# Gate projections of tiles 2 to 7 as seven block products per pair of tiles, with the low parts on GpSimd

## The chip, the cores and the metric

The kernel runs on one core of one Trainium2 chip. The metric is the device time of one execution in microseconds, the median of several; lower is better. A core has TensorE (PE in the rows, its weight loads PEld), VectorE (DVE), ScalarE (ACT), GpSimd (POOL), and SyncE (SP), whose queue here only issues transfers.

## The reference, cut to what matters

One decoder layer on 520 tokens (512 of a prompt, 8 single samples): three token mixers on one normalised input, merged by sigmoid gates, then an MLP with squared ReLU. The gates are the last 3 x 1024 columns of the input projection:

```python
def in_projection(h, norm_g, w_in, b_gate):
    xn = rmsnorm(h, norm_g)
    parts = jnp.split(xn @ w_in, SPLIT_POINTS, axis=-1)
    gates = tuple(jax.nn.sigmoid(parts[9 + i] + b_gate[i]) for i in range(N_BRANCH))
...
mixed = gates[0] * y_a + gates[1] * y_b + gates[2] * y_c
h = h + mixed @ w_out
hn = rmsnorm(h, norm_mlp_g)
return h + jnp.square(jax.nn.relu(hn @ w_up)) @ w_down
```

## The kernel before, in words

**Numbers.** Everything is float32, and TensorE gets each operand as two parts: a high (the value rounded to TensorE's format, an ACTIVATE Copy on ScalarE) and a low (value minus high). A block product is then three matmuls for each 128 x 128 weight block: high x high, high x low of the activation, low x high of it. The activation's parts are xh and xl, [128, 8 blocks, 520 tokens].

**Units and ticks.** A unit is one weight tile of 1024 x 128 (make_units, L51). It is loaded into one of WR = 3 raw slots (wraw), split by split_hi (L880) on ScalarE into one of two high slots (whi) and by split_lo on GpSimd (L836) or VectorE (L1209) into one of two low slots (wlo); LO decides which engine, in the gates and branches mostly in turn. A tick is one output tile for one half of the tokens (260), so two ticks a unit in the gates: 8 blocks x 3 = 24 matmuls into one of three PSUM banks G0 to G2 (BANK, L187). The branch units have shorter ticks: a "c" unit eight of 6 matmuls (yc of four tiles), an "ab" unit four of 12 (ya and yb of one tile). TICKS (L100) is the order, and each engine runs through the same list with its own part of each tick: TensorE project (L1712), VectorE take (L1308), ScalarE gate (L931) and others. make_plan (L290) hangs the attention's steps, the page loads of the cache and the branch splits on ticks by hand. Engines meet only at semaphores; within an engine the order of the list holds.

**Around the gates.** Tick 84 is the first gate tick (g0, tile 0, half 0). Gates come by tile, three branches each: units 42 to 53 are tiles 0 to 3. Then come "c" of tiles 0 to 3, and "ab" of tile t, each followed by the three gate units of tile t + 4; then "c" of tiles 4 to 7, and four "ab" units in a row; then eight "out" units. For a gate tick VectorE multiplies the bank by rstd into tg, and ScalarE takes the tanh in place. A branch tick of VectorE multiplies the bank by (1 + gate) into macc or mtmp and adds mtmp to macc, and after yb mix_split (L1091) and a VectorE step make mixh and mixl, the operands of "out". branch_split (L1075, L1602) makes binh and binl, the operands of "c" and "ab", from ticks 95 to 100 on. In ticks 84 to 95 TensorE also does sums over cached pages (v_sum) and smaller attention steps. x_again (L767) loads the input again into hT, to which "out" adds.

**Seven products.** In three quarters of the MLP's down projection the kernel already computes a pair of tiles as seven products instead of eight: product (L1688), with block sums on VectorE (block_sum, L1282), highs of 128 x 512 on ScalarE, three lows on GpSimd (plain_low, L850, those of unsummed blocks) and four on VectorE (sum_low), and take_product (L1256). It cuts the two tiles and the activation into 2 x 2 blocks (rows of the weights by 512, tokens by 260) and uses four sums of weight blocks and four of activation blocks.

## Time and profile before

| | us |
|---|---|
| median of 3 runs (1008.74 to 1009.38) | 1008.75 |
| the profiled execution | 1010.09 |
| its span, first to last instruction | 1006.8 |
| TensorE busy | 986.1 |
| VectorE busy | 587.9 |
| ScalarE busy | 439.8 |
| GpSimd busy | 312.6 |

Busy times are of the span. Durations on TensorE overlap, since matmuls are pipelined: a group's mean is longer than the distance between two matmuls, and the distance is to be taken from the chain or the timeline. The chain of waits goes back from the last instruction to what released it.

### The profile page before, as it was taken

Reading aid. Unit: us, or ns where it says so; the run is one execution under the profiler, and the core shown is the slowest. Engines: PE = TensorE matmul, PEld = TensorE weight load, DVE = VectorE, ACT = ScalarE, POOL = GpSimd, SP = SyncE. Lnnn points to the kernel's source line nnn. Section 1 sums busy time; section 2 is a strip of 40 time slices with the busy share of each in tenths; the row PEclk is TensorE's granted clock in tenths of the full one; section 3 lists DMA queues with packets and bytes.
Section 4 is the critical chain, followed back from the end, with each engine's and each line's share of the span. In section 5 each row is a group of like instructions: output and inputs, shape, how many; then the busy total and the mean of one; then the engine's idle time right before and its main releaser. Section 6 shows DMA issues by size and latency. Waiting matters only on the chain.

```text
span 1006.8 us, 21775 instructions
## 1 busy us (share of the span) xinstructions
PE 986.1 (98%) x8426; PEld 914.7 (91%) x8426; DVE 587.9 (58%) x1042; ACT 439.8 (44%) x858; POOL 312.6 (31%) x180
## 2 busy tenths in 40 slices
PE   7999999999999999999999999999999999999996
PEld 7988787797787787899999999999999999999995
DVE  6214478799355556253444475777847947873334
ACT  6114656677244332252233324465346436424532
POOL 2333233222312221012211112244634445354720
PEclk9999999999999999999999999999999999999999
DMA  8589977756797676624222326537576586469102
GB/s 301 181 274 320 336 260 237 289 204 207 264 334 238 224 241 202 241 84 169 89 101 85 105 89 226 204 138 266 218 262 257 215 282 250 159 261 359 61 1 85
DMA packets 65671, 209.47 MB, mean 208 GB/s; under 512 B 7833, under 2 KB 10138, under 8 KB 63266
## 3 DMA queue, kind: packets, MB, share of 16 engines
q1 hardware_dynamic: 65282, 207.75, 58.7%
q8 instruction: 67, 1.10, 0.4%
q10 hardware_dynamic: 288, 0.35, 0.2%
q14 instruction: 34, 0.28, 0.1%
HBM read 200.59 MB, written 51.48 MB: 250 GB/s over the span
## 4 chain that ended last, share of the span: by engine, by line
PE 93%; DVE 4%; issue 1%; ACT 1%; DMA 0%; DVEq 0%; ACTq 0%
PE G L1658 61%; PE S L1658 14%; PE Z L1658 13%; PE TR L1661 2%; PE OU L1658 2%; DVE pw L1496 1%; DVE mtmp L1201 1%; DMA xraw<-in_xt_dram 0%; DVE macc L1198 0%; DVE psp L1201 0%; PE TR L1658 0%; DVE share L1547 0%; DVE dvT L1198 0%; ACT mixh L878 0%; DVE pT L1505 0%
## 5 line engine op out<-in xcount | busy, mean ns | idle before, releaser
L1658 PE MATMUL G<-xh,whi 128*128 128x260 f32 x1288 | 372.3, 289 | 7.9 <-DVE xl L1201 7.2
L1658 PE MATMUL G<-xl,whi 128*128 128x260 f32 x1288 | 364.7, 283 | 0.0
L1658 PE MATMUL G<-xh,wlo 128*128 128x260 f32 x1288 | 364.4, 283 | 0.0
L844 POOL TENSOR_TENSOR wlo<-wraw,whi 128x1024 fp32r<-128x1024 f32 x60 | 148.4, 2474 | 477.2 <-ACT whi L878 477.2
L1658 PEld LDWEIGHTS G<-xh,whi 128*128 128x128 f32 x1288 | 243.5, 189 | 38.3 <-issue 32.3
L1658 PEld LDWEIGHTS G<-xl,whi 128*128 128x128 f32 x1288 | 243.7, 189 | 0.0
L1658 PEld LDWEIGHTS G<-xh,wlo 128*128 128x128 f32 x1288 | 243.6, 189 | 0.0
L878 ACT ACTIVATE whi<-wraw 128x1024 fp32r<-128x1024 f32 (+1 forms) x84 | 88.0, 1048 | 204.4 <-PE G L1658 186.0
L840 POOL TENSOR_TENSOR wlo<-mraw,whi 128x512 fp32r<-128x512 f32 x60 | 81.0, 1374 | 95.2 <-ACT whi L878 95.2
L854 POOL TENSOR_TENSOR mlow<-mraw,bhigh 128x512 fp32r<-128x512 f32 x36 | 57.9, 1626 | 66.0 <-DVE bsum L1198 58.9
L1198 DVE TENSOR_TENSOR tg<-G,rstd 128x260 f32<-128x260 f32 x48 | 20.5, 427 | 78.7 <-PE G L1658 78.7
L1198 DVE TENSOR_TENSOR slow<-bsum,bhigh 128x512 fp32r<-128x512 f32 x48 | 60.1, 1252 | 3.0 <-ACT bhigh L878 3.0
L1658 PE MATMUL S<-xl,whi 128*128 128x260 f32 x176 | 49.7, 282 | 0.0
L1658 PE MATMUL S<-xh,wlo 128*128 128x260 f32 x176 | 49.6, 282 | 0.0
L1658 PE MATMUL S<-xh,whi 128*128 128x260 f32 x176 | 49.6, 282 | 0.0
L878 ACT ACTIVATE whi<-mraw 128x512 fp32r<-128x512 f32 (+1 forms) x62 | 36.3, 637 | 25.6 <-PE G L1658 9.4
L1496 DVE TENSOR_TENSOR_SCAN pw<-psp 128x512 f32<-128x512 f32 (+3 forms) x33 | 46.4, 1406 | 1.1
L1658 PE MATMUL G<-binh,whi 128*128 128x260 f32 x160 | 45.7, 285 | 1.3 <-issue 1.3
L1658 PE MATMUL G<-binh,wlo 128*128 128x260 f32 x160 | 45.2, 283 | 0.0
L1658 PE MATMUL G<-binl,whi 128*128 128x260 f32 x160 | 45.2, 283 | 0.0
L878 ACT ACTIVATE bhigh<-bsum 128x512 fp32r<-128x512 f32 x48 | 30.2, 630 | 32.4 <-DVE bsum L1198 32.0
L936 ACT ACTIVATE tg<-tg,cvec 128x260 f32<-128x260 f32 x48 | 24.2, 505 | 45.6 <-DVE tg L1198 45.5
(329 smaller groups left out, 2227.9 us busy)
## 6 DMA issues: line engine op xcount, KB each, us to landing
wraw<-in_w_in_dram SPq DMA_DIRECT2D x65, 512.0 KB, 5.7
kv<-in_kpool_dram SPq DMA_DIRECT2D x128, 256.0 KB, 3.7
kv<-in_vpool_dram SPq DMA_DIRECT2D x128, 256.0 KB, 3.5
mraw<-in_w_up_dram SPq DMA_DIRECT2D x32, 512.0 KB, 5.7
out_win_k_kept_dram<-in_cache_win_k_dram SPq DMA_DIRECT2D x8, 2047.0 KB, 11.3
out_win_v_kept_dram<-in_cache_win_v_dram SPq DMA_DIRECT2D x8, 2047.0 KB, 11.5
mraw<-in_w_down_dram SPq DMA_DIRECT2D x30, 512.0 KB, 3.5
wraw<-in_w_ab_dram SPq DMA_DIRECT2D x8, 512.0 KB, 3.2
```

Of the source, the lines that this page charges most:

```text
L840: nc.gpsimd.tensor_tensor(low(u)[:, part], raw(u)[0][:, part], high(u)[:, part].bitcast(F32), ALU.subtract).then_inc(w_lo, 1)
L844: nc.gpsimd.tensor_tensor(low(u), raw(u)[0], high(u).bitcast(F32), ALU.subtract).then_inc(w_lo, 1)
L854: nc.gpsimd.tensor_tensor(block_low(g, j), block_raw(g, j), block_high(g, j).bitcast(F32), ALU.subtract).then_inc(b_lo_pool, 1)
L878: return nc.scalar.activation(out, in_, ACT.Copy, **kw)
L936: nc.scalar.activation(part, part, ACT.Tanh, scale=0.5, bias=bgate[:, g, t:t + 1]).then_inc(tanh_made, 1)
L1198: return nc.vector.tensor_tensor(out, a, b, op)
L1201: return nc.vector.scalar_tensor_tensor(out, a, scalar, b, op0, op1)
L1496: link(nc.vector.tensor_tensor_scan(w_[:, ::-1], l[:, ::-1], l[:, ::-1], carry, ALU.add, ALU.bypass))
L1658: return nc.tensor.matmul(out, lhsT, rhs, start=start, stop=stop, **kw)
L1661: return nc.tensor.transpose(out, in_, ident[0:rows, 0:rows])
```

## The change

Gate tiles 2 to 7 are taken in pairs of tiles (2 and 3, 4 and 5, 6 and 7) for each of three branches: nine pairs, in three batches of three. A pair is seven products of 12 matmuls; its last two come after the first product of the next pair. The first batch follows gate tile 1, the second "ab" of tile 1, the third "ab" of tile 3. ScalarE makes the seven highs of 128 x 512 in a ring of six, GpSimd all seven lows, VectorE four sums of weight blocks. Banks are shared: products 0, 2, 1, 5 follow each other in one bank, 3 and 6 in another, 4 has its own; ScalarE copies the first bank out after 0, 2 and 1, VectorE adds bank and copy and scales by rstd. Sums of the activation (xd1 to xd4, 128 x 1040 each) are made in ticks 85 to 96: six steps on GpSimd (x_odd), four on VectorE (x_even), four highs on ScalarE (x_hi) and four lows on VectorE (x_lo); the last pair overwrites a quarter of xh and xl. The branch splits 0 to 3 come ten ticks earlier, the page loads at the end of the attention every 2.5 ticks instead of 3, and x_again waits for the last gate product. Several tiles move in SBUF, which changes no instruction of theirs.

```diff
-    for t in range(4):
+    for t in range(2):
         gates(t)
+    gate_pairs(2)
     for half in range(2):
         unit("c", half, "w_c", half, KC, [("yc", 2 * i, 2, "dil", 4 * half + i) for i in range(4)])
         for t in range(4 * half, 4 * half + 4):
             unit("ab", t, "w_ab", t, KC, [("ya", 0, 4, "conv", t), ("yb", 4, 4, "sb", t)])
-            if half == 0:
-                gates(t + 4)
+            if t in (1, 3):
+                gate_pairs(t + 3)
...
+GSEQ = (0, 4, 2, 3, 1, 5, 6)
...
+            _seven = [(_u, ("gprod", 0, KC // 2, None, _q), _j, _j == 6) for _j in GSEQ]
+            TICKS += _seven[:1] + _late + _seven[1:5]
+            _late = _seven[5:]
...
+G_HIGHS, G_SUM_RING = 6, 6
...
+    if _q % 3:
+        _k = [gate_tick(_q - 1, n) for n in range(7)]
+        _ticks = (_k[1:7] + [_next], [_k[1], _k[1], _k[3], _k[4]], [_k[1], _k[2], _k[3], _k[4], _k[5], _k[6], _next])
+    elif _q == 0:
+        _ticks = ([_f - 3] * 3 + [_f - 2] * 2 + [_f - 1, _next], [_f - 4, _f - 4, _f - 3, _f - 3], [_f - 3, _f - 3, _f - 2, _f - 2, _f - 2, _f - 1, _next])
+    else:
+        _ticks = ([_f - 6, _f - 6, _f - 5, _f - 4, _f - 4, _f - 3, _next], [_f - 6, _f - 6, _f - 5, _f - 4], [_f - 6, _f - 6, _f - 5, _f - 4, _f - 4, _f - 3, _next])
...
-        v_ticks.append(v_ticks[-1] + 3)
+        v_ticks.append(v_ticks[-1] + 2.5)
...
+    for n in range(2):
+        add(t + 2.5 * n, "x_odd", n)
+        add(t + 3 + n, "x_even", n)
+    for n in range(3):
+        add(v_end + 3 + 0.5 * n, "x_hi", n)
+        add(v_end + 3 + 0.5 * n, "x_lo", n)
+    add(GATED_TICK - 0.5, "x_hi", 3)
+    add(GATED_TICK - 0.5, "x_lo", 3)
+    add(gate_tick(GPAIRS - 1, 6) + 1, "x_again")
...
+            def x_odd(n):
...
+                for i, (a, b, op) in enumerate(((ah, bh, ALU.subtract), (out, al, ALU.add), (out, bl, ALU.subtract))):
+                    if i:
+                        pool.wait_ge(xd_odd, 3 * n + i)
+                    nc.gpsimd.tensor_tensor(out, a, b, op).then_inc(xd_odd, 1)
...
+            def gate_low_pool(q, n):
+                j = G_POOL[n]
...
+                pool.wait_ge(g_hi, 7 * q + GSEQ.index(j) + 1)
...
+                nc.gpsimd.tensor_tensor(gate_low(q, j), gate_raw(q, j), gate_high(q, j).bitcast(F32),
+                                        ALU.subtract).then_inc(g_lo_pool, 1)
...
+            def gate_seven(k, q, j):
+                b, t = gate_tiles(q)
+                if j in (0, 2, 1):
+                    if j == 0 and b == 0:
+                        await_gate_parts(act, t)
+                    act.wait_ge(made, k + 1)
+                    copy(gate_part(t + (j > 0), b, j % 2), bank[BANK[k]][:, 0:HALF]).then_inc(g_copied, 1)
+                if j not in (0, 2, 3):
...
+                    nc.scalar.activation(part, part, ACT.Tanh, scale=0.5, bias=bgate[:, b, tile:tile + 1]).then_inc(tanh_made, 1)
+
+            def gate_hi(q, n):
+                j = GSEQ[n]
...
+                m = 7 * q + n - G_HIGHS
+                if m >= 0:
+                    act.wait_ge(made, gate_tick(m // 7, m % 7) + 1)
+                copy(gate_high(q, j), gate_raw(q, j)).then_inc(g_hi, 1)
...
+            def take_gate(k, q, j):
+                if j not in (4, 1, 5, 6):
+                    return
...
+                if j != 5:
+                    dve.wait_ge(g_copied, 3 * q + (4, 6, 1).index(j) + 1)
+                dve.wait_ge(made, k + 1)
+                if j == 5:
+                    tt(dst, src, root, ALU.mult).then_inc(dve_took, 1)
+                    return
...
+                tt(dst, src, dst, ALU.add).then_inc(dve_took, 1)
+                dve.wait_ge(*took(k))
+                tt(dst, dst, root, ALU.mult).then_inc(g_scaled, 1)
...
+            def gate_product(k, part, q, j):
+
+                if part == 0:
+                    pe.wait_ge(g_lo_pool, 7 * q + G_POOL.index(j) + 1)
+                    if q == 0 and j in (1, 2, 3, 6):
+                        pe.wait_ge(xd_lo, (2, 3, 6, 1).index(j) + 1)
+                    if j in (2, 1, 5):
+                        pe.wait_ge(g_copied, 3 * q + (2, 1, 5).index(j) + 1)
+                    elif j == 6:
+                        pe.wait_ge(*took(at("gprod", q, 1)))
+                    else:
+                        pe.wait_ge(*took(PREV[k]))
+                out = bank[BANK[k]][:, 0:HALF]
+                act_h, act_l = gate_act(j)
+                for kc in range(part * KC // 4, (part + 1) * KC // 4):
+                    wh, wl = gate_high(q, j)[:, kc, :], gate_low(q, j)[:, kc, :]
+                    mm(out, wh, act_h[:, kc, :], kc == 0 and j in (0, 4, 3), False, skip_group_check=True)
+                    mm(out, wh, act_l[:, kc, :], False, False, skip_group_check=True)
+                    ins = mm(out, wl, act_h[:, kc, :], False, kc == KC // 2 - 1, skip_group_check=True)
```

## Rows read from the trace of the kernel before

**Rows 1.** The page's sections 1 and 2: busy time by engine, granted clock.
```profile
PE 986.1 (98%) x8426; PEld 914.7 (91%) x8426; DVE 587.9 (58%) x1042; ACT 439.8 (44%) x858; POOL 312.6 (31%) x180
...
PEclk9999999999999999999999999999999999999999
```

**Rows 2.** Chain that ended last, in order of time: start us, us, what.
```profile
392.88 8.85 PE G L1658 x72
...
431.44 39.51 PE G L1658 x330
471.64 107.19 PE G L1658 x894
...
699.37 1.44 PE Z L1658 x12
```

**Rows 3.** Windows: stretch, us, busy (count) of PE, PEld, DVE, ACT, POOL, clock.
```profile
470.00:600.00 130.00, 128.66 (x1067) 127.80 (x1066) 70.81 (x123) 40.48 (x56) 26.36 (x11) 1.00 0.31 104
```

**Rows 4.** The same chain in the last four "ab" units.
```profile
582.93 0.42 DVE mtmp L1201
583.36 0.02 issue
583.38 0.44 DVE macc L1198
```

**Rows 5.** Groups of instructions by shape, 390 to 600: busy us, mean ns, idle before.
```profile
L844 POOL TENSOR_TENSOR wlo<-wraw,whi 128x1024 fp32r<-128x1024 f32 x17 | 40.7, 2392 | 174.5 <-ACT whi L878 174.5
...
L1198 DVE TENSOR_TENSOR tg<-G,rstd 128x260 f32<-128x260 f32 x48 | 20.5, 427 | 78.7 <-PE G L1658 78.7
L1198 DVE TENSOR_TENSOR macc<-macc,mtmp 128x260 f32<-128x260 f32 x32 | 19.7, 616 | 1.1
L1198 DVE TENSOR_TENSOR wlo<-wraw,whi 128x1024 fp32r<-128x1024 f32 x16 | 19.6, 1223 | 7.2 <-ACT whi L878 7.2
...
L1198 DVE TENSOR_TENSOR binl<-convy,binh 128x520 fp32r<-128x520 f32 x4 | 2.6, 695 | 1.1 <-ACT binh L878 1.1
...
L936 ACT ACTIVATE tg<-tg,cvec 128x260 f32<-128x260 f32 x48 | 24.2, 505 | 45.6 <-DVE tg L1198 45.5
```

**Rows 6.** Timeline of GpSimd, then of VectorE, 476 to 480.5: start us, us.
```profile
476.73 2.40 POOL L844 TENSOR_TENSOR wlo<-wraw,whi 128x1024 fp32r<-128x1024 f32 x1 [10.04 <-ACT whi L878]
...
477.49 1.92 DVE L1198 TENSOR_TENSOR macc<-macc,mtmp 128x260 f32<-128x260 f32 x1
479.44 0.42 DVE L1201 SCALAR_TENSOR_TENSOR mtmp<-tg,G 128x260 f32<-128x260 f32 x1
479.90 0.43 DVE L1198 TENSOR_TENSOR macc<-macc,mtmp 128x260 f32<-128x260 f32 x1
```

**Rows 7.** Timeline of VectorE, then of GpSimd, in a seven-product pair of the down projection.
```profile
697.50 0.69 DVE L1198 TENSOR_TENSOR bsum<-mraw,bsum 128x512 f32<-128x512 f32 x1
698.10 0.42 DVE L1198 TENSOR_TENSOR hT<-hT,Z 128x260 f32<-128x260 f32 x1
...
700.15 1.44 DVE L1198 TENSOR_TENSOR slow<-bsum,bhigh 128x512 fp32r<-128x512 f32 x1
...
701.86 1.44 DVE L1198 TENSOR_TENSOR slow<-bsum,bhigh 128x512 fp32r<-128x512 f32 x1
...
701.01 1.73 POOL L854 TENSOR_TENSOR mlow<-mraw,bhigh 128x512 fp32r<-128x512 f32 x1
```

**Rows 8.** Timeline of GpSimd in the up projection: two lows, VectorE not on SBUF.
```profile
743.37 2.56 POOL L840 TENSOR_TENSOR wlo<-mraw,whi 128x512 fp32r<-128x512 f32 x2 [3.17 <-ACT whi L878]
```

**Rows 9.** The page's section 5: the highs of the block sums on ScalarE.
```profile
L878 ACT ACTIVATE bhigh<-bsum 128x512 fp32r<-128x512 f32 x48 | 30.2, 630 | 32.4 <-DVE bsum L1198 32.0
```

**Rows 10.** Timeline: GpSimd's low of unit 44; VectorE's take of tick 95.
```profile
397.20 2.39 POOL L844 TENSOR_TENSOR wlo<-wraw,whi 128x1024 fp32r<-128x1024 f32 x1 [17.62 <-ACT whi L878]
...
434.45 0.43 DVE L1198 TENSOR_TENSOR tg<-G,rstd 128x260 f32<-128x260 f32 x1 [3.33 <-PE G L1658]
```

**Rows 11.** The page's section 6: issues, KB each, median us to landing.
```profile
wraw<-in_w_in_dram SPq DMA_DIRECT2D x65, 512.0 KB, 5.7
...
kv<-in_vpool_dram SPq DMA_DIRECT2D x128, 256.0 KB, 3.5
...
hT<-in_xt_dram SPq DMA_DIRECT2D x1, 2080.0 KB, 8.3
```

More of the change, by code:

```diff
@@ L189 @@
 FIRST, LEAD = 4, 4
-_opened = UP_TICK
+_opened = 3
+_free = [RING[(GATED_TICK + _n) % GBANKS] for _n in range(GBANKS)]
 for _k in range(NT):
@@ L211 @@
 for _u, _unit in enumerate(UNITS):
-    HI.append(sum(0 if seven(u) else 1 + halved(u) for u in range(_u + 1)))
-    if seven(_u):
+    HI.append(sum(0 if seven(u) or gated(u) else 1 + halved(u) for u in range(_u + 1)))
+    if seven(_u) or gated(_u):
         LO.append(None)
@@ new lines, in x_lo, with gate_sum @@
+            def x_lo(n):
+                dve.wait_ge(xd_hi, n + 1)
+                if n == 3:
+                    hi, lo, full_ = xh[:, 0:4, half(1)], xl[:, 0:4, half(1)], xd1
+                else:
+                    i = (1, 2, 0)[n]
+                    hi, lo, full_ = xdh[:, i], xdl[:, i], (xd2, xd3, xd4)[n]
+                tt(lo, full_[:], hi.bitcast(F32), ALU.subtract).then_inc(xd_lo, 1)
+            def gate_sum(q, n):
+                i = G_SUMS[n]
+                even, odd = raw(U_GATE[q]), raw(U_GATE[q] + 1)
+                top, end = slice(0, KC // 2), slice(KC // 2, KC)
+                if q == 0 and n == 0:
+                    dve.wait_ge(xd_lo, 3)
+                    dve.wait_ge(bin_lo, 4)
+                if n == 0:
+                    dve.wait_ge(*even[1:])
+                    dve.wait_ge(*odd[1:])
+                if q == 1 and n == 0:
+                    dve.wait_ge(bin_hi, 9)
+                m = 4 * q + i - G_SUM_RING
+                if m >= 0:
+                    dve.wait_ge(made, at("gprod", m // 4, SUM_AT[m % 4]) + 1)
+                if n:
+                    dve.wait_ge(g_summed, 4 * q + n)
+                first, second = gate_raw(q, SUM_AT[0]), gate_raw(q, SUM_AT[1])
+                a, b, op = ((odd[0][:, top], odd[0][:, end], ALU.add), (first, even[0][:, top], ALU.subtract),
+                            (even[0][:, top], odd[0][:, top], ALU.subtract), (even[0][:, end], second, ALU.subtract))[i]
+                tt(gate_raw(q, SUM_AT[i]), a, b, op).then_inc(g_summed, 1)
@@ L1371, in take @@
                     dve.wait_ge(made, k + 1)
-                    m = macc[:, tile, half(h)]
+                    m = macc[tile // 4][:, tile % 4, half(h)]
                     gate = tg[tile % 4][:, g, half(h)]
```

289 lines of the change are left out of this document (229 added, 60 removed).

## The prediction

> **What bounds the kernel now.** I read the page's busy times first: TensorE is busy for 98% of the span, GpSimd for 31%, and the granted clock is 0.9 or more in every slice [rows 1], which is the upper level, 2.4 GHz. Busy shares don't say who sets the end, so the chain of waits comes next, merged and in order of time: through the gates it is TensorE alone, 330 matmuls in 39.51 us and then 894 in 107.19 us without a break [rows 2]. That gives the price of one 128x128x260 matmul, 39.51/330 = 0.1197 us. The stretch 470 to 600 confirms it: TensorE 128.66 of 130 us, VectorE 70.81, ScalarE 40.48, GpSimd 26.36 [rows 3]. So here work removed from TensorE is time won, as long as three engines that are now half idle or more can carry what is put on them. The only place where the chain leaves TensorE is the run of four "ab" units at the end, where it sits on VectorE's mtmp and macc steps, 0.42 and 0.44 us apart [rows 4].
>
> **The edit on TensorE.** A pair of gate tiles is now 2 tiles x 2 token halves x 8 blocks x 3 = 96 matmuls; as seven products of 4 blocks x 3 it is 84. Nine pairs save 9 x 12 = 108 matmuls, 108 x 0.1197 = 12.9 us. Nothing is added on TensorE. That seven products can run at this price is seen in the down projection, 12 matmuls in 1.44 us [rows 2]. Within a pair TensorE then takes 84 x 0.1197 = 10.05 us instead of 11.5.
>
> **What the other engines get, per pair.** GpSimd: seven lows of 128x512 instead of one 128x1024 (the other of the pair is VectorE's). Alone such a low takes 2.56/2 = 1.28 us [rows 8]; seven are 9.0 us of the 10.05. ScalarE: seven highs of 0.63 us [rows 9], three copies of 128x260 (not in the trace; between the 0.39 that a high of this size would take in proportion and the 0.50 us of a tanh [rows 5]; I take 0.4) and four tanh, about 7.5 us; it fits, but only in order. VectorE loses a 1.22 us low and two multiplies, and gets four block sums of 0.69 [rows 7], four adds of 0.43 and three extra scalings of 0.43: about 6 us. By counts all fits. It fits badly because VectorE and GpSimd can't both work on SBUF.
>
> **The lock.** Look at GpSimd's low from 476.73 to 479.13 [rows 6] and at VectorE's macc<-macc,mtmp beside it: it takes 1.92 us, ends just after 479.13, and the same instruction right after takes 0.43 [rows 6]. The group's mean is 616 ns [rows 5]. The multiply of PSUM by rstd never shows this (mean 427 [rows 5]). In the seven-product stage it works both ways: VectorE's slow<-bsum,bhigh take 1.44 us, GpSimd's low 1.73 instead of 1.28, and one of each goes by every 1.71 us (700.15 to 701.86) [rows 7]. Two back-to-back sums are 0.60 apart (697.50, and the next instruction at 698.10), so I price a 128x512 VectorE step at 0.60 of a shared resource and a GpSimd low at 1.71 - 0.60 = 1.11. In the same manner: 1024 elements on GpSimd 2.39 - 0.15 = 2.25, 1040 elements 2.28, on VectorE 1.15 and 1.17 (from 1.22), 520 elements 0.65 and 260 elements 0.35 (from 695 and 430 ns) [rows 5, 6].
> The Trainium skill says the same thing of this pair in SBUF — State Buffer, "SBUF: two separate sides": the port pair that VectorE and GpSimd share is an exclusive lock, taken by a two-SBUF-input VectorE instruction or a GpSimd one for its whole length. The trace agrees (1.92 against 0.43 us). It speaks against this change, and GPSIMD Engine Reference, "Engine selection", does too, since it advises VectorE for elementwise work and calls GpSimd about twice as slow on two inputs (here 2.39 against 1.22 us). Without the lock the sum would be the whole 12.9 us.
>
> **Per pair the lock is overbooked**: 7 x 1.11 + 4 x 0.60 + 3 x 0.35 = 11.2 us against TensorE's 10.05. Only a lead, lows made before a batch of three pairs begins (at most six highs exist at once), can bridge that. So I count the lock over each batch.
>
> **Batch 1 with what leads to it.** The count begins when GpSimd starts the low of unit 44 at 397.20 [rows 10]. Until product 6 of the third pair can run, the lock must have served on GpSimd: two unit lows 4.5, x_odd 6 x 2.28 = 13.7, 21 lows 23.3, the low of the "c" unit, which stands before the last low, 2.25: 43.75 us. On VectorE: two unit lows 2.3, ten branch lows 6.5, x_even and x_lo 8 x 1.17 = 9.4, 12 sums 7.2, 8 scalings 2.8: 28.2 us. Together 72 us, so 469.2 at the earliest. TensorE ends the last tick of gate tile 1 at 434.4 [rows 10] and would want that product after 20 others and two short "yc" ticks, 28.7 + 1.4 later, at 464.6. Stall: at least 4.6 us. The bound from below takes a lock that never idles; it will idle while ScalarE and VectorE hand each other the ten branch splits and the x sums in ticks 91 to 96, and I add 1. The far end is some 5 us more.
>
> **Batches 2 and 3.** From six ticks of 12 matmuls (6 x 1.44 = 8.6 us) before a batch, where its first highs are due, to its last product there are 38.8 us. The lock needs 21 lows 23.3, 12 sums 7.2, 8 scalings 2.8, six macc adds 2.1, two mixl 1.3, one unit low 1.15: 37.9 us. It just fits. But two "ab" units now stand together ahead of each batch, and there VectorE has, in 8.6 us, six mtmp 2.5, six adds 2.6, two mixl 1.4 and four sums 2.7 = 9.2 us, with six lows (6.7 us of lock) to dodge: 9.2 + 6.7 - 8.6 - 2.9 (two banks of slack) = 4.4 us at worst, 0 at best. I take 1.5 for each batch, as the alternate pattern of [rows 7] hides about two thirds, and 0.4 for the short ticks behind batches 1 and 3.
>
> **Edits at nothing.** The weights keep three raw slots; a tile lands 5.7 us after issue [rows 11], an odd tile's slot comes free with the second low of the pair before, some 8 us ahead of its sum; if that cover goes, 1 us a pair. SyncE's load of hT now waits for the last gate product with weight loads behind it; 8.3 us [rows 11] lie under 28 us of "c" and "ab" work. Page loads at 2.5 instead of 3 ticks each land in 3.5 us [rows 11] under a step of 9. The moved tiles of the MLP cost nothing.
>
> **Sum.** 12.9 - (4.6 + 1.0) - 2 x 1.5 - 0.4 = 3.9 us won. The profiled execution took 1010.09 us (span 1006.8), so it would be 1006.2; it stands 1.3 above the median of the timed runs, 1008.75, and from that the forecast is **1004.9 us** (this case: 1001.5 to 1006.7).
>
> **Rivals.** (1) *The lead covers nearly all.* If a low holds the lock for less than 1.11, or VectorE slips into the 0.17 us that GpSimd leaves between two lows, batch 1 stalls 2 us or less: 996 to 1001, say 998. For it: the down stage keeps TensorE at 1.44 us per product with VectorE almost full. Against: only three lows per pair are GpSimd's there.
> (2) *No change.* The hand-overs of ticks 91 to 96 leave the lock idle longer: ScalarE must do x_hi 3 (over 1 us) before it can copy product 0's bank, which product 2 waits for; x_lo 3 must be done for product 1. With 4 us for that, 1008.9.
> (3) *Slower: ScalarE's order holds a bank.* After product 3 ScalarE goes to the high of the next pair's product 2, and stands there until VectorE's second sum. Behind product 4 VectorE has an add 0.43, a scaling and two sums, each of which may first wait 1.11 for a low: 0.43 + 1.46 + 1.71 + 1.71 = 5.3 us, against the 4.3 us of three products. So the copy of product 1's bank comes 1.0 + 0.63 + 0.4 = 2.0 us after its end, while product 5 wants the bank after 1.44: 0.6 a pair; product 4 of the next pair, whose bank frees with VectorE's take of product 5, adds 0.3. Nine pairs x 0.9 = 8 us: **1012.9**. It decides from 3.9/9 = 0.43 us a pair. For it: 11.2 us of lock per 10.05 means that VectorE's steps meet a low nearly each time. Against: in a batch's first pair GpSimd is capped by the ring of highs and leaves gaps.
> (4) *The lock alone*: a rule taken at its word, every pair at 11.2 us and no lead, wins 9 x (11.5 - 11.2) = 2.7 us less 5.6 for the x sums: 1011.7. It belongs to (3) in the chances; the Trainium skill's page on SBUF, as cited, is the rule.
> That the change doesn't do what it says can be left out: 84 matmuls a pair stand in the code.
>
> **Chances.** Forecast 0.33, rival (1) 0.15, (2) 0.20, (3) with (4) 0.32. A difference of 0.2%, 2 us, is about what a measurement of this kernel can tell from no change. Faster by more: 0.33 + 0.15 = 0.48; within: 0.20; slower: 0.32. The range cuts the upper half of (1) and the tail of (3), where all nine pairs wait 1.2 us or more: 998.5 to 1014. The likeliest case's own is 1001.5 to 1006.7.
>
> **What would show it.** 8318 matmuls instead of 8426. GpSimd's lows of 128x512 in the gates at 1.5 to 1.75 us each (1.3 would speak for rival 1). TensorE idle 4 to 7 us between 410 and 470, released by GpSimd's low or a VectorE step; under 2 us in products inside batches 2 and 3, over 4 us if rival 3 holds, then released by ScalarE's copy of G. The time from the first "out" tick to the end is unchanged. The prediction is wrong if TensorE has no gaps there, or if its gaps end with a weight load.

## The result, and the profile after

The changed kernel takes **1031.88 us** (median of 4 runs, 1030.99 to 1033.51) beside 1008.95 for the kernel before on the same chip: 1.0229 times as long, 95% interval 1.0211 to 1.0246. It is 22.9 us slower, where 3.9 us less had been forecast, and it lies outside the range. The saved matmuls are gone as counted, so 22.9 + 12.9 = 35.8 us were lost elsewhere.

The page, sections 1 and 2, as [rows 1]:

```profile
PE 983.5 (96%) x8318; PEld 906.9 (88%) x8318; DVE 663.6 (64%) x1104; ACT 467.7 (45%) x934; POOL 402.4 (39%) x240
...
PEclk9999999999999999999999999999999999999998
```

There are 8318 matmuls instead of 8426. TensorE's share fell by two points only, VectorE and GpSimd are still under two thirds, and nothing on this page looks like a bound. The windows tell more (columns: stretch, us, busy and count of PE, PEld, DVE, ACT, POOL, then clock, DMA share, GB/s). They are the lead-in with batch 1, one round of batch 2 with the two "ab" units behind it, and two short stretches; [rows 3] is a stretch of the same place before:

```profile
386.00:470.00 84.00, 74.29 (x598) 65.05 (x595) 65.14 (x68) 35.98 (x66) 48.67 (x26) 0.96 0.38 130
501.50:550.60 49.10, 43.66 (x349) 42.21 (x349) 38.72 (x53) 23.23 (x47) 33.18 (x22) 1.00 0.26 87
447.00:449.00 2.00, 1.28 (x6) 1.31 (x7) 1.66 (x2) 0.58 (x2) 0.69 (x1) 0.54 0.00 0
449.00:452.00 3.00, 3.00 (x21) 3.00 (x21) 2.83 (x5) 2.35 (x5) 1.27 (x1) 0.74 0.00 0
```

A round holds 348 matmuls, 41.7 us at 0.1197, and takes 49.1; VectorE is busy for 38.7 of them and GpSimd for 33.2. Behind the last gate product nothing changed: from the first matmul on mixh, the start of the "out" units, to the end of the span it is 409.3 us (from 619.97) against 409.6 (from 597.24).

**Where TensorE stood.** These are the first matmuls after its longest waits, in the timeline (start us, us, engine, what, count, idle before and who ended it): the first three products of batch 1, the "c" unit's second tick, and the first pair of batch 2 up to the ends of its pairs.

```profile
438.20 0.39 PE L1948 MATMUL G<-xh,ghigh 128*128 128x260 f32 x1 [1.55 <-POOL glow L1029]
...
442.11 0.36 PE L1948 MATMUL G<-xh,ghigh 128*128 128x260 f32 x1 [2.20 <-DVE tg L1424]
...
447.72 0.56 PE L1948 MATMUL G<-xdh,ghigh 128*128 128x260 f32 x1 [3.94 <-POOL gslow L1029]
...
479.44 0.36 PE L1948 MATMUL G<-binh,whi 128*128 128x260 f32 x1 [2.05 <-issue]
...
501.52 0.36 PE L1948 MATMUL G<-xh,ghigh 128*128 128x260 f32 x1 [0.81 <-DVE mtmp L1427]
...
505.90 0.36 PE L1948 MATMUL G<-xdh,ghigh 128*128 128x260 f32 x1 [1.24 <-ACT tg L1055]
...
511.57 0.39 PE L1948 MATMUL G<-xh,ghigh 128*128 128x260 f32 x1 [0.61 <-POOL glow L1029]
...
523.15 0.39 PE L1948 MATMUL G<-xh,ghigh 128*128 128x260 f32 x1 [0.90 <-POOL glow L1029]
```

Tick 95 ended at 434.4 before. After two products, 2.9 us, the third could start at 437.3; it starts at 447.72, 10.4 late: 2.2 had been lost when tick 95 ended (436.65), 7.7 are the three waits above. The rest of the ledger goes by the time between first matmuls, less 0.1197 us for each matmul between them. It is 1.3 us because the third product ran at the lower clock (the fourth starts 2.74 us after it instead of 1.44, with the 0.54 and 0.74 above), 5.3 in the rest of batch 1 and its "c" unit, 2.7 in the two "ab" units behind it, 7.4 in the round of batch 2, and 8.6 from there to the first "out" tick, where the kernel before loses 1.9 that are taken off. About 4 of these 8.6 belong to the second "c" unit (a wait of 2.1, then a clock of 0.69 to 0.93). Together that is 35.7 of 35.8, and each of batches 2 and 3, with the waits ahead of it, costs some 7.

**One pair at its steady pace.** GpSimd, then VectorE, then the high on ScalarE that GpSimd waits for at 527.54:

```profile
515.49 4.24 POOL L1029 TENSOR_TENSOR gslow<-gsum,ghigh 128x512 fp32r<-128x512 f32 x3 [1.29 <-ACT ghigh L1055]
519.72 5.07 POOL L1029 TENSOR_TENSOR glow<-wraw,ghigh 128x512 fp32r<-128x512 f32 x3
524.76 1.49 POOL L1029 TENSOR_TENSOR gslow<-gsum,ghigh 128x512 fp32r<-128x512 f32 x1
527.54 4.17 POOL L1029 TENSOR_TENSOR gslow<-gsum,ghigh 128x512 fp32r<-128x512 f32 x3 [1.29 <-ACT ghigh L1055]
```

```profile
518.50 1.78 DVE L1424 TENSOR_TENSOR gsum<-wraw 128x512 f32<-128x512 f32 x1
520.39 1.58 DVE L1424 TENSOR_TENSOR gsum<-gsum,wraw 128x512 f32<-128x512 f32 x1
522.07 1.57 DVE L1424 TENSOR_TENSOR gsum<-wraw,gsum 128x512 f32<-128x512 f32 x1
523.57 0.42 DVE L1424 TENSOR_TENSOR tg<-G,tg 128x260 f32<-128x260 f32 x1
524.02 1.06 DVE L1424 TENSOR_TENSOR tg<-tg,rstd 128x260 f32<-128x260 f32 x1
525.01 1.79 DVE L1424 TENSOR_TENSOR gsum<-wraw 128x512 f32<-128x512 f32 x1
```

```profile
526.83 0.63 ACT L1055 ACTIVATE ghigh<-gsum 128x512 fp32r<-128x512 f32 x1 [1.20 <-DVE gsum L1424]
```

From 515.49 to 527.54 is one pair: 12.05 us for TensorE's 10.05. (TensorE's own distance between two first products is 11.58 here, 511.57 to 523.15, since some lows were made ahead of the batch.) GpSimd is busy for 10.8 of the 12.05. Every sum of VectorE in this stretch, 0.69 us alone, takes 1.6 to 1.8, because it lets one low go first (over the round the three kinds of sum have means of 1.42, 1.28 and 0.99, so some meet none); the step that reads PSUM (523.57) takes its 0.42. The fourth sum, which may start only behind these, begins at 525.01 just behind a low's start, ends at 526.80, its high ends at 527.46, and for this GpSimd stands 1.29 us. The two engines take turns and then wait for each other once a pair.

### The profile page after: what moved, and what is told of

It reads as the page before. It is cut to its first block, busy times and chain, and to the rows that moved or that the text cites. A ratio compares the mean times of both kernels' runs of the same rounds, so it can differ in the third digit from the quotient of the medians.

```text
span 1029.2 us, 21949 instructions
## 1 busy us (share of the span) xinstructions
PE 983.5 (96%) x8318; PEld 906.9 (88%) x8318; DVE 663.6 (64%) x1104; ACT 467.7 (45%) x934; POOL 402.4 (39%) x240
## 4 chain that ended last, share of the span: by engine, by line
PE 80%; DVE 8%; issue 4%; POOL 4%; ACT 2%; DMA 1%; SPq 0%; DVEq 0%; ACTq 0%; POOLq 0%
PE G L1948 50%; PE S L1948 14%; PE Z L1948 11%; POOL gslow L1029 3%; PE TR L1951 2%; PE OU L1948 2%; DVE binl L1424 1%; POOL glow L1029 1%; DVE xd L1424 1%; DVE tg L1424 1%; ACT ghigh L1055 1%; DVE mtmp L1427 1%; DMA xraw<-in_xt_dram 1%; DVE pw L1784 1%; DVE wlo L1424 1%
## 5 line engine op out<-in xcount | busy, mean ns | idle before, releaser
L1948 PE MATMUL G<-xh,whi 128*128 128x260 f32 x992 | 289.6, 292 | 8.7 <-DVE xl L1427 7.4
L1948 PE MATMUL G<-xl,whi 128*128 128x260 f32 x992 | 282.0, 284 | 0.0
L1948 PE MATMUL G<-xh,wlo 128*128 128x260 f32 x992 | 281.6, 284 | 0.0
L990 POOL TENSOR_TENSOR wlo<-wraw,whi 128x1024 fp32r<-128x1024 f32 x51 | 128.3, 2515 | 359.6 <-ACT whi L1055 359.6
L1948 PEld LDWEIGHTS G<-xh,whi 128*128 128x128 f32 x992 | 188.4, 190 | 40.1 <-issue 32.9
L1948 PEld LDWEIGHTS G<-xh,wlo 128*128 128x128 f32 x992 | 188.4, 190 | 0.0
L1948 PEld LDWEIGHTS G<-xl,whi 128*128 128x128 f32 x992 | 188.4, 190 | 0.0
L1029 POOL TENSOR_TENSOR gslow<-gsum,ghigh 128x512 fp32r<-128x512 f32 x36 | 51.0, 1430 | 22.6 <-ACT ghigh L1055 13.7
L1948 PE MATMUL G<-xh,ghigh 128*128 128x260 f32 x144 | 42.6, 296 | 11.8 <-POOL glow L1029 5.8
L1029 POOL TENSOR_TENSOR glow<-wraw,ghigh 128x512 fp32r<-128x512 f32 x27 | 41.4, 1556 | 28.1 <-ACT ghigh L1055 25.0
```

Source lines behind the costliest of these rows:

```text
L990: nc.gpsimd.tensor_tensor(low(u), raw(u)[0], high(u).bitcast(F32), ALU.subtract).then_inc(w_lo, 1)
L1029: nc.gpsimd.tensor_tensor(gate_low(q, j), gate_raw(q, j), gate_high(q, j).bitcast(F32), ALU.subtract).then_inc(g_lo_pool, 1)
L1948: return nc.tensor.matmul(out, lhsT, rhs, start=start, stop=stop, **kw)
```

## The experiments

"Before" is the kernel before, measured beside each run on the same chip; its medians lie between 1008.61 and 1009.41. The differences to the kernel after that follow are between medians of separate sets of executions, mostly on another chip, so they are good to about 1 us. The first four runs had two executions each, the others four to six. All change the kernel after unless said otherwise.

| run | us | before | ratio (95%) |
|---|---|---|---|
| e1 lows on half | 1016.86 | 1008.82 | 1.005 to 1.011 |
| e2 small x sums | 1025.90 | 1008.82 | 1.014 to 1.020 |
| e3 four lows on VectorE | 1026.81 | 1008.82 | 1.015 to 1.021 |
| e4 x_odd on VectorE | 1028.68 | 1008.82 | 1.017 to 1.023 |
| e5 bank | 1024.91 | 1009.09 | 1.015 to 1.018 |
| e6 ring | 1029.08 | 1009.09 | 1.018 to 1.021 |
| e7 all mended | 1016.84 | 1009.09 | 1.006 to 1.010 |
| e8 tiles 4 to 7 | 1019.50 | 1009.09 | 1.009 to 1.012 |
| e9 early entry | 1035.25 | 1008.96 | 1.025 to 1.028 |
| e10 six, x sums spread | 1026.46 | 1008.96 | 1.016 to 1.022 |
| e11 six, pairs between | 1036.80 | 1008.96 | 1.026 to 1.030 |
| e12 nine, all and early | 1017.23 | 1008.96 | 1.006 to 1.010 |
| e13 copies for sums | 1029.94 | 1008.61 | 1.019 to 1.022 |
| e14 light | 1002.73 | 1008.61 | 0.993 to 0.997 |
| e15 v pages | 1030.43 | 1008.61 | 1.021 to 1.024 |
| e16 six, all mended | 1016.46 | 1009.41 | 1.005 to 1.008 |
| e17 three, all mended | 1013.65 | 1009.41 | 1.003 to 1.006 |

### How much hangs on GpSimd's lows and on the x sums

```diff
-gate_low(q, j), gate_raw(q, j), gate_high(q, j).bitcast(F32)
+gate_low(q, j)[:, 0:2], gate_raw(q, j)[:, 0:2], gate_high(q, j)[:, 0:2].bitcast(F32)
```

> The changed kernel (1031.9 us, 23 slower than the one before), but each of GpSimd's 63 gate lows works on half of its elements (128x256), and TensorE multiplies with the written half twice, so the low parts of these products are not right; matmuls, waits and order are as they were. Theory A (throughput: the lows hold the SBUF lock that VectorE and GpSimd share, 11.2 us for a pair of 10.05): a low falls from 1.11 to about 0.55 us of lock, a pair to 7.3, the waits of TensorE inside batches 2 and 3 (5.5 us each in the changed kernel's trace) nearly go: 31 to 36 us of stalls become about 20, so 1015 to 1019. Theory B (order: what TensorE waits for are hand-overs VectorE to ScalarE to GpSimd at a batch's start and the x sums ahead of the first): 1027 to 1030, since only the last link of each chain is 0.6 us shorter.

It leaves half of each low out (the products read the written half twice). 15.0 us came off, as theory A had it. Its round in the same window view:

```profile
498.84:542.91 44.07, 43.22 (x348) 42.09 (x349) 28.48 (x53) 23.43 (x47) 20.14 (x22) 1.00 0.29 96
```

44.07 us instead of 49.10, with VectorE's busy time down by 10.2 us although not one of its instructions changed: that was time in which it stood before GpSimd's lows. Batch 1's entry hardly moved: the third product starts at 447.12 instead of 447.72, after a wait of 4.1 us, and the profile names ScalarE's copy for it:

```profile
447.12 0.56 PE L1948 MATMUL G<-xdh,ghigh 128*128 128x260 f32 x1 [4.09 <-ACT tg L1055]
```

```diff
-nc.gpsimd.tensor_tensor(out, a, b, op).then_inc(xd_odd, 1)
+nc.gpsimd.tensor_tensor(out[:, :, 0:8], a[:, :, 0:8], b[:, :, 0:8], op).then_inc(xd_odd, 1)
```

The same for x_even, x_hi and x_lo: the sums of the activation cover 8 of 260 columns, and the products read x itself.

> The changed kernel with the steps that make the activation's block sums (six on GpSimd, four on VectorE, the highs and lows of the four) cut from 260 columns to 8 in each row; the products of the sums take other parts of the activation instead, so they are not right. Theory B (the lead-in): the third product starts 10.4 us late in the changed kernel, plus 1.5 us of lower clock behind it; both go except about 2 us: 1021 to 1023. Theory A: the lock has 23 us less to serve ahead of the first batch, but batches 2 and 3 stay as they are: 1022 to 1025 too; what tells them apart is the place, under A TensorE's waits for lows inside the first batch go as well (3 us more).

6.0 us less, outside the times of both theories (1021 to 1023, 1022 to 1025). The third product started at 441.48 instead of 447.72, still after a wait of 3.1 us. The place speaks for theory B: the waits for lows inside the first batch stayed (1.38 us at 460.65), and a round of batch 2 still took 49.1. The x sums cost 6 us in the place that the change gave them.

### Who does the lows

```diff
+for q, n in GLOW_DVE_AFTER.get(k, []):
+    gate_low_dve(q, n)          # lows of the sums 2, 3, 1, 5; GpSimd keeps 0, 4, 6
```

> The changed kernel with the four lows of summed blocks of each pair on VectorE, as in the down projection, and three on GpSimd. Theory A: VectorE holds the lock 0.60 us for a low and GpSimd 1.11, so a pair falls from 11.2 to 9.2 us of lock, under TensorE's 10.05: waits inside batches fall by a half or more, 1022 to 1026. Theory B: VectorE's list gets 36 steps longer, it is late already at each batch's start, and the copies and highs of ScalarE behind it come later: 1031 to 1036. No wait is added for TensorE but the one for a low by its new maker.

5.1 us less, 0.8 above theory A's range. By turns a pair would fall by 4 x (1.28 - 0.60) = 2.7 us, from 12.05 to under TensorE's 10.05, 18 us for nine; most of that didn't come. GpSimd now stood for ScalarE's highs for 93.6 us between 386 and 610 (its plain and sum lows together 50.7 in the kernel after), and product 0 of a pair still waited 0.6 for its low.

```diff
-nc.gpsimd.tensor_tensor(out, a, b, op).then_inc(xd_odd, 1)
+tt(out, a, b, op).then_inc(xd_odd, 1)       # x_odd among VectorE's stages
```

> The changed kernel with the six x_odd steps on VectorE (1.24 us each) instead of GpSimd (2.9 each). Theory A: 13.7 us of lock become 7.0, and VectorE's steps no longer wait for GpSimd's in ticks 85 to 91: the lateness of 10.4 us at the third product falls to 4 to 6, so 1026 to 1028. Theory B, order alone: VectorE has 7.4 us more to do in a stretch where TensorE waits for it: 1031 to 1036.

3.2 us less, 0.7 above theory A's range. The third product still waited until 445.44.

### Banks and rings

```diff
-            if _late and (_job[0] == "ya" or _h):
+            if _late:
```

> After kernel with one edit: the two late products (5, 6) of a batch's last pair stand behind the first yc tick of the c unit instead of the second, as they already do behind the first ya tick. Theory A (a held bank): at the c unit two of three banks belong to pending products, so the second yc tick must wait 2.3 to 2.4 us for VectorE's take of the first, in batches 1 and 3; with the edit both gaps go, and what the lowered clock costs behind them: 1032 - 4 to 5 = about 1027.5. Rival B (VectorE is simply behind there, since its sums and adds meet GpSimd's lows): the wait moves to another tick of the same place and the time falls by at most 1: 1031.

7.0 us less, more than theory A had: both waits at the "c" units are gone (4.2), and the clock behind the second stays at 1.00 (in the kernel after 0.69 from 586 to 589 and 0.93 from 589 to 600). What held the tick at 479.44 is seen on VectorE in the kernel after; the take of the first "yc" tick, macc, stands behind a unit's low, and the second tick has no other bank:

```profile
477.35 0.52 DVE L1424 TENSOR_TENSOR tg<-tg,rstd 128x260 f32<-128x260 f32 x1
477.79 1.21 DVE L1424 TENSOR_TENSOR wlo<-wraw,whi 128x1024 fp32r<-128x1024 f32 x1
478.93 0.41 DVE L1427 SCALAR_TENSOR_TENSOR macc<-tg,G 128x260 f32<-128x260 f32 x1
```

```diff
+    _ticks[0][6] = _k[6] if _q % 3 else _f      # the high of product 6, was _next
```

> After kernel with one edit: ScalarE makes the high of a pair's last product (6) one product earlier, behind product 6 of the pair before (in a batch's first pair behind product 0), instead of together with the high of the next pair's product 0. GpSimd's work and VectorE's are the same. Theory A (order): GpSimd idles for a high and then has two lows in a row before the next pair's product 0, which waits 0.9 to 1.2 us in each of the six second and third pairs; with the edit these gaps go, 5 to 7 us, about 1026. Rival B (the lock between VectorE and GpSimd is the bound of a pair, 11.2 us of lock to 10.05 of TensorE): no change beyond 1 us, 1031 to 1032.

2.8 us less, so theory A holds for a part only, and rival B's 1 us is passed too. The profiled execution was the slowest of the five (1034.04; the others 1027.86 to 1029.14), so its rows show where the waits stand and not where the 2.8 us were won. The waits moved: a round of batch 2 takes 48.64 us instead of 49.1, and the second pair's first product, released at 511.57 in the kernel after, no longer waits, but the third's waits longer than at 523.15:

```profile
526.88 0.39 PE L1949 MATMUL G<-xh,ghigh 128*128 128x260 f32 x1 [1.39 <-POOL glow L1030]
```

> After kernel with five edits together: the bank edit, the ring edit, the four sum lows of a pair on VectorE, x_odd on VectorE, and the step of the last v pages as before (3 ticks at the end instead of 2.5). Theory A (separate order and lead-in waits, that add up): the parts measured alone took 5.1 and 3.2 off; with about 4 and 6 for bank and ring and 1.7 for the clock dip around 392: 1032 - 20 = about 1012, with 4 us for overlap between them 1016. Rival B (one shared resource): the savings replace each other, and it stays at 1022 to 1027.

15.0 us less (e3, e4, e5, e6 and e15 together; alone they gave 5.1 + 3.2 + 7.0 + 2.8 + 1.5 = 19.6). They add up to three quarters, which is theory A with its 4 us of overlap (1016). The round still takes 47.85 us, now with GpSimd busy for 16.2 of them and VectorE for 39.8. From the second pair's first product to the third's it is now 10.40 us (503.49 to 513.89). The same distance was 11.58 in the kernel after, 11.30 with the four lows alone (e3), 11.59 with the ring edit alone (e6) and 10.44 with half lows (e1): neither edit does it by itself, both together do. But at the start of the batch TensorE waits 1.13, 0.68, 0.45 and 1.14 us within 7.3 us, for VectorE's last "ab" steps and for ScalarE's copy. So here the round no longer loses most in its pairs, but at the entry of the batch.

### Is it the place, or the amount

```diff
-        _ticks = ([_f - 6, _f - 6, _f - 5, _f - 4, _f - 4, _f - 3, _next], ...
+        _ticks = ([_f - 9, _f - 8, _f - 8, _f - 7, _f - 6, _f - 5, _next], ...
```

> After kernel with one edit: the sums, highs and lows of the first pair of batches 2 and 3 stand 8 to 5 ticks ahead of the batch instead of 6 to 3, so that they don't fall together with the last ab steps on VectorE. Theory A (entry: VectorE falls behind because four sums stand among the last ab steps): the gaps at the start of each batch (1.1 + 1.5 + 0.6 us) shrink by half, 3 to 4 us for two batches: 1028. Rival B (the entry is held by the ab steps themselves and by ScalarE's mixh, which stands before the copy of product 0's bank): within 1 us of 1031.9. Third (the lows then hold the lock under more of the ab steps): the gaps move ahead of the batch, 1031 to 1034.

The third answer had the mechanism; the time, 1035.25, lies 1.3 above its range, and the executions overlap with those of the kernel after (1032.35 to 1036.12 against 1030.99 to 1033.51). The waits at the start of the batch shrank, and these came ahead of it, inside the "ab" units (first matmuls of three ticks):

```profile
495.33 0.36 PE L1948 MATMUL G<-binh,whi 128*128 128x260 f32 x1 [1.95 <-issue]
...
499.18 0.36 PE L1948 MATMUL G<-binh,whi 128*128 128x260 f32 x1 [0.65 <-issue]
...
503.00 0.35 PE L1948 MATMUL G<-binh,whi 128*128 128x260 f32 x1 [2.14 <-issue]
```

The round stays at 49.29 us: in this move the waits changed their place and not their sum. One such move doesn't show that every order would lose as much.

> All nine pairs, with all edits so far together: bank, ring, four sum lows and x_odd on VectorE, v pages as before, early entry. The run without the early entry took 1016.8. Theory A (entries of batches 2 and 3, some 3.9 us each there): 1012 to 1014. Rival B: 1016 to 1017. What is left against 1008.9 would be the lead-in of batch 1, with its gap of 4 us.

1017.23 against 1016.84: the early entry brings nothing here either.

```diff
-    for t in range(2):
+    for t in range(4):
         gates(t)
-    gate_pairs(2)
```

> Only the gates of tiles 4 to 7 (six pairs, 72 matmuls fewer than before) as seven products, GpSimd making all lows; tiles 2 and 3 as before, c unit behind them; bank and ring edit in it. The x sums then have the work of tiles 2 and 3 and two ab units, some 45 us, beside them. Theory A (about half of the loss is the lead-in of batch 1, with what follows from it): nothing is lost there; 72 x 0.1197 = 8.6 saved, less 1.2 + 3.5 in each of two batches: 1008.9 - 8.6 + 9.4 = about 1009.5, between 1005 and 1012. Rival B (every pair costs the same, (1032 - 1009)/9 = 2.6 us): 1008.9 + 6 x 2.6 = 1024, less what bank and ring give.

1019.5, above theory A by 10 and below B by 4. My price of a round, 4.7 us, was taken from single waits of the kernel after; its round is really 7 us too long, and here, with the bank and the ring mended, still some 7, as the x sums and x_lo 3 leave 4.6 us of waits too (1.2 at 436, 2.3 at the "c" unit, 1.1 behind).

```diff
-        add(t + 2.5 * n, "x_odd", n)
+        add(x0 + 3 * n, "x_odd", n)     # x0: one tick into the gates of tile 2
```

> As the run with tiles 4 to 7 only, and beside bank and ring: the four sum lows on VectorE, the early entry, and the x sums moved from under the attention's end to the ticks of the gates of tiles 2 and 3. Theory A (chains of hand-overs at the entries, x sums in the way at the c unit, GpSimd's seven lows of 1.5 us plus 1.3 us of waiting in a pair of 10.05 us): 1019.5 less 2.3 (c unit), 1 a pair (6), 2 for the entries: 1009, between 1006 and 1012. Rival B (the number of elements on VectorE and GpSimd together is what counts, wherever they stand): 1016 to 1020.

It was worse by 7 us than e8 (its four executions spread from 1025.11 to 1031.62), and both theories missed. In the gates of tiles 2 and 3 nothing had been waiting, and the x sums put this there (GpSimd, then TensorE):

```profile
451.47 2.44 POOL L1022 TENSOR_TENSOR xd<-xh 128x1040 f32<-128x1040 f32 x1
453.99 4.88 POOL L1022 TENSOR_TENSOR xd<-xd,xl 128x1040 f32<-128x1040 f32 x2
458.83 3.32 POOL L995 TENSOR_TENSOR wlo<-wraw,whi 128x1024 fp32r<-128x1024 f32 x1
```

```profile
462.20 0.59 PE L1963 MATMUL G<-xh,whi 128*128 128x260 f32 x1 [5.39 <-POOL wlo L995]
```

The unit's low stands in GpSimd's order behind three x sums. Two more waits, of 3.2 and 4.9 us, follow in the branch units; the first stands behind two lows of the x sums on VectorE, the second behind x_hi 3 and x_lo 3, which are themselves behind a high that waits 5.1 us for an early sum. In this order the x sums cost more where there seemed to be room than under the attention's end; since the early entry and the lows on VectorE came in the same run, their shares aren't parted.

```diff
-            if t in (1, 3):
-                gate_pairs(t + 3)
+            if t in (1, 2):
+                gate_pairs(4, [t - 1])
+            if t == 3:
+                gate_pairs(4, [2])
+                gate_pairs(6)
```

> As the run before it, but the three pairs of tiles 4 and 5 are not in one batch: the first stands behind ab 1, the second behind ab 2, the third with the pairs of tiles 6 and 7 behind ab 3. Theory A (a pair alone between ab units has its seven lows and four sums in the 15.8 us of both, and one entry of two falls away): 2 to 4 us below the run before it, 1005 to 1007, which is faster than the kernel before. Rival B (each pair behind an ab unit pays an entry of its own, about 3 us): 3 us above it.

It went the way of rival B and further: 10.3 us above e10 by the medians, 5.8 in the profiled executions, where B had 3. The pair behind "ab" 2 and the last batch each waited 2.5 us (526.94 and 548.02) for ScalarE's copy of their first bank, the pair behind "ab" 1 only 0.5. In my order of the highs one of them stood before that copy and waited for VectorE's fourth sum. That is a fault of this order, so the run doesn't show what a better one would give.

> Tiles 4 to 7 as pairs (six), with bank, ring, four sum lows and x_odd on VectorE, v pages as before. Nothing of the x sums is moved from under the attention's end. Theory A (loss per batch about 6 us, beside its two ab units, x sums covered there for about 3): 1008.9 - 8.6 + 12 + 3 = 1015, 1012 to 1016. Rival B (the edits add up as in the nine-pair kernel, 15 off): 1019.5 - 10 = 1009.5.

```diff
-            if t in (1, 3):
-                gate_pairs(t + 3)
+            if t == 1:
+                gate_pairs(4)
+            if t in (2, 3):
+                gates(t + 4)
```

> Only tiles 4 and 5 as pairs (three pairs, 36 matmuls fewer), the rest as before, with the same edits. Theory A: 1008.9 - 4.3 + 6 + 3 = 1013.5, slower than the kernel before at any number of pairs. Rival B (the x sums and most of the waits lie under the other work once only one batch is left): 1004.6 + 3 = 1007 to 1008, at last not slower than before.

1016.46 and 1013.65, within 1.5 us of theory A both. (In e17 the gates of tiles 6 and 7 are computed from the x that the last x sum has already overwritten.) With 3, 6 and 9 pairs the edited kernels save 4.3, 8.6 and 12.9 us and lose, by these medians, 8.5, 15.7 and 21.2 (e12): the first batch costs 8.5 us, the second 7.2 more and the third 5.5 more, against 4.3 saved by each. No number of batches paid in these kernels.

### What is left without the work, what the turns are, and the clock

> After kernel with all of it made light together: lows on half their elements, sums as copies, x sums and their splits on 8 of 260 columns, bank edit, v pages as before; the output is not the reference's. TensorE's matmuls are the same. Theory A (the saving is there and only covered by waits for the two engines): 1008.9 - 12.9 = 996, up to 1000 for the waits that stay. Rival B (products of 12 matmuls cost more than their count, at their changes of bank and weights): 1003 or more with hardly a gap.

1002.73 (executions from 1000.80 to 1006.41), 5.9 below before: above theory A's range and just below rival B's 1003. The saving is there, but not whole. Rival B's reason doesn't hold: most products start 1.43 to 1.44 us after the one before, which is their count. A pair takes 10.45 us (442.53 to 452.98) rather than 10.05 because two of the seven distances are longer, 1.52 and 1.74 us, the latter with a short wait for a low; in other pairs that wait is one for ScalarE's copy. The third product of batch 1 still waits 1.8 for the copy. The window from 386 to 600 has TensorE busy for 209.2 of 214 us, against 188.7 in the kernel after:

```profile
386.00:600.00 214.00, 209.22 (x1734) 198.14 (x1734) 122.62 (x239) 97.73 (x183) 72.08 (x78) 1.00 0.37 126
```

```diff
-tt(gate_raw(q, SUM_AT[i]), a, b, op).then_inc(g_summed, 1)
+nc.vector.tensor_copy(gate_raw(q, SUM_AT[i]), a).then_inc(g_summed, 1)
```

> After kernel, but VectorE's four block sums of each pair are copies of their first block (one SBUF input instead of two, same size and place), so the output is not the reference's. GpSimd's work and the order of all engines stay. Theory A (VectorE and GpSimd take turns at SBUF, one two-input step of VectorE per low): the lows fall from about 1.5 to 1.3 us, the copies take under 0.6 us and don't wait, a batch with its two ab units takes 44 to 46 us instead of 49, in all 1019 to 1023. Rival B (GpSimd's seven lows in order and their waits for ScalarE bound the pair, whatever VectorE does): 1028 to 1031.

1.9 us less, in rival B's range. Theory A's own test failed, and for a reason that the rows show: a copy with one input takes its turn too. Alone it takes 0.42, beside a low 1.5 (VectorE):

```profile
519.74 0.42 DVE L1577 COPY gsum<-wraw 128x512 f32<-128x512 f32 x1
520.27 1.49 DVE L1577 COPY gsum<-gsum 128x512 f32<-128x512 f32 x1
521.86 1.33 DVE L1577 COPY gsum<-wraw 128x512 f32<-128x512 f32 x1
...
525.78 1.53 DVE L1577 COPY gsum<-wraw 128x512 f32<-128x512 f32 x1
```

A pair still takes 11.86 us (GpSimd's lows at 513.68 and 525.54), and GpSimd stands 2.5 of them for highs. So this run can't part the turns from the order of waits: VectorE was busy for 4.5 us less in a round, and the round became only 0.7 shorter, as rival B has it. e1 is the one that shows the turns, in VectorE's busy time; how much of a pair's 12.05 us is turns and how much is the order of the hand-overs stays open.

```diff
-        v_ticks.append(v_ticks[-1] + 2.5)
+    v_ticks = v_ticks[:PAGES - 5] + [77.5, 80, 84, 86, 87.5]
```

> After kernel with one edit: the last v pages stand at the ticks of the kernel before (3 ticks apart at the end, not 2.5). In the kernel after, TensorE stood for 1.0 us twice between 386 and 393 us and ran 24 matmuls in 4.62 us at a granted clock of 0.51 to 0.64, which the kernel before did not. Theory A (that step caused the dip): 1.7 us less, 1030.2. Rival B (the dip comes with anything near that place, or is given back before product 0 of the first pair because that waits for GpSimd anyway): 1031.9 within 0.6.

1030.43; the runs of both overlap (1029.64 to 1032.41 against 1030.99 to 1033.51), so the sum of both effects is small. The early dip is gone (390 to 394: clock 1.00 instead of 0.82) and the third product starts 1.5 us earlier, at 446.22; but now the clock falls from 438 on:

```profile
438.00:447.00 9.00, 3.77 (x19) 3.32 (x18) 4.80 (x6) 4.34 (x8) 5.79 (x4) 0.67 0.17 58
447.00:452.00 5.00, 5.00 (x27) 5.00 (x27) 3.94 (x6) 2.66 (x6) 2.77 (x2) 0.58 0.09 20
```

## Why the prediction was wrong, by its steps

**The edit on TensorE: right, but for short waits in each pair.** 108 matmuls fewer at 0.1197 apart within a product. With the other engines' work made light a pair takes 10.45 us (e14), not 10.05: nine times 0.4, 3.6 us, had no term. They are not the price of changing product or bank, since most products follow at 1.44, but short waits at two places of each pair.

**The lock per pair: right in kind, mis-sized.** I took a low's share as 1.71 - 0.60 = 1.11 from a stage in which low and sum alternate. That difference counts the start of the next step as free. The pair's 12.05 us, less 4 x 0.60 + 3 x 0.35, leave 8.6 for seven lows and GpSimd's one standstill: 1.23 each, near the 1.28 of a low alone [rows 8]. With 1.28 and no overlap the sum would have been 12.4. The trace had both numbers, and I took the lower. The 0.60 of a sum was low too: the second step of that row reads PSUM, and in the kernel after, where each sum waits for the one before, two with no low beside them start 0.71 apart (435.56 and 436.27). The lows took 1.43 (of sums) and 1.56 us (plain) in the mean, below and at the lower end of the forecast 1.5 to 1.75.

**"Only a lead can bridge that", and it was counted over a batch: the step that failed, for batches 2 and 3.** The count over a batch (37.9 of 38.8 us) made each of batches 2 and 3 cost 1.5; they cost some 7 each. A count of throughput needs a queue in which work can be done ahead. Here the highs stand in a ring of six, the fourth sum waits for a product of the pair before, and each engine runs in order, so VectorE meets a low at nearly every step and GpSimd then waits for VectorE's last sum. With 12.4 a pair, the same count gives 37.9 + 21 x 0.17 = 41.5 of 38.8 and would have warned. What the runs show is that less work on the lows helps (e1, a round of 44.07 instead of 49.10) and that an earlier start of the first pair doesn't (e9). Inside a batch both the lows and the order count: a pair fell from 11.58 to 10.40 us only when four lows went to VectorE and the high of product 6 came earlier (e7), and hardly when one of the two was done (e3, e6).

**Batch 1: the sum of 5.6 stands against some 17 (10.4 + 1.3 + 5.3), as large a miss.** Ten of these are lost before the third product, and the step that failed is the 1.0 for "hand each other the ten branch splits and the x sums". Rival (2) had the mechanism: these hand-overs, and ScalarE's x_hi 3 ahead of the copy of product 0's bank. ScalarE in the kernel after:

```profile
442.00 0.51 ACT L1113 ACTIVATE tg<-tg,cvec 128x260 f32<-128x260 f32 x1 [3.20 <-DVE tg L1424]
442.42 1.14 ACT L1055 ACTIVATE ghigh<-gsum 128x512 fp32r<-128x512 f32 x2
443.46 0.62 ACT L1055 ACTIVATE binh<-o_dT 128x520 fp32r<-128x520 f32 x1
445.32 0.51 ACT L1113 ACTIVATE tg<-tg,cvec 128x260 f32<-128x260 f32 x1 [1.24 <-DVE tg L1424]
445.73 0.61 ACT L1055 ACTIVATE ghigh<-gsum 128x512 fp32r<-128x512 f32 x1
446.25 1.05 ACT L1055 ACTIVATE xh<-xd 128x1040 fp32r<-128x1040 f32 x1
447.21 0.37 ACT L1055 ACTIVATE tg<-G 128x260 f32<-128x260 f32 x1
```

VectorE beside it:

```profile
439.87 1.75 DVE L1424 TENSOR_TENSOR binl<-o_dT,binh 128x520 fp32r<-128x520 f32 x1
441.55 0.42 DVE L1424 TENSOR_TENSOR tg<-G,rstd 128x260 f32<-128x260 f32 x1
444.11 0.83 DVE L1424 TENSOR_TENSOR binl<-o_dT,binh 128x520 fp32r<-128x520 f32 x1 [2.15 <-ACT binh L1055]
444.87 0.41 DVE L1424 TENSOR_TENSOR tg<-G,rstd 128x260 f32<-128x260 f32 x1
```

The copy ends at 447.58 and the third product starts at 447.72. The profile names GpSimd's low there, which ends at 447.69; but this product's own low is the one of 439.34, done at 441.1, so by the code's waits it was the copy; in e2, where x_hi 3 is short, the profile itself names the copy, for 3.1 us. And the copy was late because the two engines handed to and fro, each in its order. VectorE's take of tick 94 came at 441.55, behind branch lows of 1.64 and 1.75 us beside GpSimd's lows; ScalarE's tanh of tick 94 (442.00) stood for it, then two highs and binh (443.46); VectorE stood 2.15 us for that binh, and behind its low came the take of tick 95 (444.87, where it was at 434.45 before), then ScalarE's tanh, a high, x_hi 3 and at last the copy. x_hi 3 is 1.05 us of this. GpSimd's lows were not the bound of it: with half lows (e1) the two branch lows took 1.25 and 0.69 us, and from the take of tick 93 to the copy it was still 10.7 us (435.93 to 446.61) instead of 12.0 (435.22 to 447.21). No run changed the order of these steps alone. I priced this chain at 1.0, the rival at 4; it and the waits before it were 7.7 of TensorE's time.

**The "c" units: no term at all.** 0.4 was set for "short ticks". Two late products hold two of three banks while short ticks need two (e5: 7.0 us with the clock). That belongs beside rival (3), which looked for a held bank, but at another place.

**Edits at nothing.** Weight loads, hT and the MLP's moved tiles: no wait on them at all, right. The page loads: a dip of the clock near 392 that I hadn't priced; 1.5 us there, little in the end.

**The rivals.** Rival (3)'s place, ScalarE's copies in the middle of a pair, waits 0.3 to 0.4 once a pair, less than the 0.6 it had. By the signs I had set, TensorE stood 9.5 us between 410 and 470 (4 to 7 forecast) and 3.5 inside the products of batch 2 behind its first (1.24, 0.28, 0.61, 0.90 and 0.43 us), 2.0 of them for ScalarE's copy and 1.5 for lows: between "under 2" and rival (3)'s "over 4". The reality was its sign with the mechanisms of (2), (4) and the bank together. I held them as alternatives that exclude each other; they were separate waits on one path, and they added. Rival (4) "at its word" with the right price, 12.05 for every pair, alone gives 1010.1 - 1.3 + 9 x 0.55 + 5.6 = 1019, outside my range.

## What to carry to other kernels

When two engines take turns at one memory, price each step at its full time alone, here 7 lows and 7 steps in a row, and ask of every pair, not of the whole, whether it fits; average over more only what the rings let run ahead. Follow one product's operands and one bank through every engine's order before trusting a sum of busy times, above all at the first and the last product of a group. And where several waits lie at different places of one chain, add them up; they aren't rivals.

## What the runs showed of the hardware

- VectorE's copies with a single SBUF input take turns with GpSimd as two-input steps do: 128x512 in 0.42 us alone, 1.33 to 1.53 beside a low (e13). The Trainium skill (SBUF — State Buffer, "SBUF: two separate sides") names both kinds of step, two SBUF inputs or a two-port performance mode, and counts a float32 copy from SBUF to SBUF among the second, so its rule fits these rows; I had read it as one of two inputs only. GpSimd's 1040-element steps took 2.9 and 3.0 us in the mean with VectorE at work beside them; with VectorE idle one took 2.44 (e10, 451.47), in line with the estimate of 2.28 for its share.
- TensorE's granted clock was 1.00 from 438 to 447, while it stood for 2.2 and 3.9 us, and 0.54, then 0.74 right behind (1.0 and 0.5 are its levels of 2.4 and 1.2 GHz); 0.69 behind that of 586. In e15 it was already 0.67 from 438 to 447. So the waits of 2.2 and 3.9 us were followed by 1.3 us more in the third product (2.74 instead of 1.44), and e5 got 7.0 us for the 4.2 of waits it took away.
